# Sample attention in blocks of four heads, with page copies between the passes of the sums

## The reference, cut to what matters

```python
z = einsum('bqhd,bkhd->bhqk', q, k) * scale + bias
mask = key_pos[None, :] < qpos[:, None]
log_1mb = where(mask, log_sigmoid(-z), 0.0)
after = cumsum(log_1mb, axis=3, reverse=True) - log_1mb
w = where(mask, exp(log_sigmoid(z) + after), 0.0)
out = einsum('bhqk,bkhd->bqhd', w, v)
```

## Time and profile before

| what | value |
|---|---|
| median of 3 runs | 1071.79 us (1070.54 to 1072.94) |
| the profiled execution | 1072.91 us, its span 1071.2 us |
| PE busy over the span | 933.6 us (87%) |
| DVE, ACT busy | 635.5 us, 443.1 us |
| mean granted TensorE clock | 0.935 |

### The profile page before, as it was taken

One profiled execution on the slowest core, in us unless ns is written; L12 is line 12 of the kernel. 1 busy time (PEld: TensorE's weight loads), 2 busy tenths in 40 slices (PEclk: granted clock), 3 DMA queues, 4 the chain that ended last, 5 costly groups with the idle time before them and its releaser, 6 DMA issues.

```text
span 1071.2 us, 12096 instructions
## 1 busy us (share of the span) xinstructions
PE 933.6 (87%) x4149; PEld 674.0 (63%) x4149; DVE 635.5 (59%) x1206; ACT 443.1 (41%) x664; POOL 40.0 (4%) x75
## 2 busy tenths in 40 slices
PE   6799999999978687874769995999999999999695
PEld 3477676777745354442347684887887887787373
DVE  2319996011053753453354726888888888987774
ACT  0210112032223232332342222778778777777642
POOL 4000000300000000000000001000000000000300
PEclk9899999999966799997889997899999999999988
DMA  8042354424040386784602310899999999998601
GB/s 236 1 148 88 114 195 146 171 79 157 1 157 1 88 315 213 258 313 157 214 2 91 110 48 9 331 338 333 336 340 344 330 336 343 332 329 321 216 16 35
DMA packets 64211, 203.30 MB, mean 190 GB/s; under 512 B 8761, under 2 KB 9081, under 8 KB 60055
## 3 DMA queue, kind: packets, MB, share of 16 engines
q1 hardware_dynamic: 55424, 185.19, 48.3%
q10 hardware_dynamic: 6031, 9.19, 2.6%
q0 software_dynamic: 2704, 8.27, 2.5%
HBM read 188.96 MB, written 14.03 MB: 190 GB/s over the span
## 4 chain that ended last, share of the span: by engine, by line
PE 46%; DVE 12%; ACT 7%; issue 3%; DVEq 0%; ACTq 0%; POOL 0%
PE bank L1999 9%; PE bank L2001 8%; PE bank L2000 8%; PE bank L1990 5%; PE bank L2095 4%; PE bank L1921 3%; PE bank L1886 2%; PE bank L1895 2%; DVE last_piece L1494 2%; ACT pieces L627 1%; ACT att L627 1%; ACT last_piece L627 1%; DVE ring_lo L1469 1%; DVE scratch L1276 1%; PE bank L1839 1%
## 5 line engine op out<-in xcount | busy, mean ns | idle before, releaser
L1711 PE MATMUL bank<-scratch,ring 128*128 128x320 f32 x896 | 242.5, 433 | 0.0
L1711 PEld LDWEIGHTS bank<-scratch,ring 128*128 128x128 f32 x896 | 169.8, 190 | 70.6 <-issue 0.5
L1494 DVE TENSOR_TENSOR pieces<-ring,pieces 128x1024 fp32r<-128x1024 f32 x141 | 168.4, 1221 | 31.8 <-ACT pieces L627 29.7
L627 ACT ACTIVATE pieces<-ring 128x1024 fp32r<-128x1024 f32 x144 | 147.6, 1059 | 19.0 <-PE bank L2001 14.1
L627 ACT ACTIVATE proj<-bank 128x512 f32<-128x512 f32 (+4 forms) x73 | 36.3, 506 | 155.4 <-PE bank L1711 117.1
L1121 DVE SCALAR_TENSOR_TENSOR proj<-scratch,par_w,proj 128x256 f32<-128x256 f32 x240 | 73.7, 380 | 1.1
L1494 DVE TENSOR_TENSOR last_piece<-ring,last_piece 128x1024 fp32r<-128x1024 f32 x47 | 57.4, 1222 | 11.5 <-ACT last_piece L627 9.7
L627 ACT ACTIVATE last_piece<-ring 128x1024 fp32r<-128x1024 f32 x48 | 51.0, 1063 | 7.2 <-PE bank L2001 7.2
L627 ACT ACTIVATE scratch<-bank 128x512 f32<-128x512 f32 (+5 forms) x42 | 19.9, 520 | 73.2 <-PE bank L1921 35.5
L1886 PE MATMUL bank<-ident,ring 128*128 128x128 f32 x256 | 35.8, 302 | 13.9 <-ACT proj L627 6.2
L2095 PE MATMUL bank<-pick_t,h_tok 128*128 128x256 f32 x320 | 43.6, 295 | 3.1 <-DVE pick_t L1487 3.1
(11 more groups left out here) (386 smaller groups left out, 1660.2 us busy)
## 6 DMA issues: line engine op xcount, KB each, us to landing
ring<-in_w_expert_gate SPq DMA_DIRECT2D x16, 2048.0 KB, 7.7
ring<-in_w_expert_up SPq DMA_DIRECT2D x16, 2048.0 KB, 7.9
ring<-in_w_expert_down SPq DMA_DIRECT2D x16, 2048.0 KB, 7.9
ring<-in_w_in SPq DMA_DIRECT2D x14, 2048.0 KB, 7.9
ring<-in_cache_k SPq DMA_DIRECT2D x64, 256.0 KB, 5.1
ring<-in_cache_v SPq DMA_DIRECT2D x64, 256.0 KB, 5.5
moe_rows<-att ACTq DMA_DIRECT2D x16, 512.0 KB, 3.7
ring<-in_w_branch SPq DMA_DIRECT2D x3, 2048.0 KB, 9.2
```

Of the source, the lines that this page charges most:

```text
L627: return F(out, in_, ACT.Copy)
L1494: TT(piece_of[r % 4][:, 1, :], raw_piece(STEP + 3 * e, r), piece_of[r % 4][:, 0, :].bitcast(F32), ALU.subtract).then_inc(s("lo_ready"), 1)
L1711: m = MM(bank[t % 4][:, 0:T], slot(j, DC, GROUP)[:, k, (t % 4) * P:(t % 4 + 1) * P], h[:, k, :], start=k == 0, stop=k == DC - 1)
```

## The change

Three things are edited. First, the products of the sample attention are cut into blocks of four heads: request `u` and head group `g` have an output of 32 rows (`quarter(u, g)`), so the stationary tile has 32 columns and there are four such tiles side by side. A score block adds up only the two head pairs of its group; a value block has only the 256 value columns of its group. `o_rows` is 256 wide, and two transposes turn it instead of four. Second, VectorE's page copies 4 and 5 move into `later_sums`: copy 4 stands between the mask and the scan, copy 5 between the scan and the subtraction, and `mask_weight` moves behind copies 6 and 7. Third, ScalarE's `exp_weight` moves behind its page copies 4 and 5.

```diff
@@ ScalarE
                 k_copy(i, 2)
                 k_copy(i, 3)
-                exp_weight(i + (-1))
                 k_copy(i, 4)
                 k_copy(i, 5)
+                exp_weight(i + (-1))
                 biased(i, 0)
                 k_copy(i, 6)
                 k_copy(i, 7)
-                copy(o_rows, bank[7][:, :]).then_inc(s("turned_copied"), 1)
+                copy(o_rows, bank[7][:, 0:256]).then_inc(s("turned_copied"), 1)
@@ VectorE
-            def later_sums(i):
+            def later_sums(i, k_between=()):
...
                 ch(TT(probs[:, PAST:KEYS], probs[:, PAST:KEYS], mask_of(i), ALU.mult))
+                for k in k_between[0:1]:
+                    k_copy(i + 1, k)
                 ch(dve.tensor_tensor_scan(terms[:, KEYS - 1::-1], ones[:, 0:1].broadcast_to((P, KEYS)), probs[:, KEYS - 1::-1], 0.0, ALU.mult, ALU.add))
+                for k in k_between[1:2]:
+                    k_copy(i + 1, k)
                 TT(scores[:, 0:KEYS], scores[:, 0:KEYS], terms[:, 0:KEYS], ALU.subtract).then_inc(s("pw_arg"), 1)
...
-                later_sums(i + (-1))
-                k_copy(i, 4)
-                k_copy(i, 5)
-                mask_weight(i + (-1))
+                later_sums(i + (-1), (4, 5))
                 k_copy(i, 6)
                 k_copy(i, 7)
+                mask_weight(i + (-1))
                 outputs(i + (-1))
@@ TensorE
+            def quarter(u, g, at_=0):
+                return slice(at_ + u * DH + g * 32, at_ + u * DH + g * 32 + 32)
+
+            def own_queries(u, c):
+                return q_cur[:, u, c * 64 + c // 2 * 32:c * 64 + c // 2 * 32 + 32]
...
-                    for c in range(WC):
-                        for u in range(2):
-                            m = MM(bank[2 + hf][rows_of[u], :], q_cur[:, u, c * 64:(c + 1) * 64], k_feat[:, u, c, :],
-                                   start=c == 0, stop=c == WC - 1)
+                    for j in range(2):
+                        for g in range(2):
+                            for u in range(2):
+                                m = MM(bank[2 + hf][quarter(u, g), :], own_queries(u, 2 * g + j), k_feat[:, u, 2 * g + j, :],
+                                       start=j == 0, stop=j == 1)
...
-                    for u in range(2):
-                        m = MM(bank[7][u * DH:(u + 1) * DH, :], probs_t[:, p * P + u * DH:p * P + (u + 1) * DH],
-                               slot(first + u, NPAGE, W)[:, p, :] if p < NPAGE else v_tok[:, 2, :],
-                               start=p == 0, stop=p == NPAGE)
+                    for g in range(2):
+                        for u in range(2):
+                            v = slot(first + u, NPAGE, W)[:, p, :] if p < NPAGE else v_tok[:, 2, :]
+                            m = MM(bank[7][quarter(u, g), 0:256], probs_t[:, quarter(u, g, p * P)], v[:, 256 * g:256 * (g + 1)],
+                                   start=p == 0, stop=p == NPAGE)
...
-                for c in range(WC):
-                    m = TR(bank[1][:, c * P:(c + 1) * P], o_rows[:, c * P:(c + 1) * P], ident[:, :])
+                for j in range(2):
+                    m = TR(bank[1][:, j * P:(j + 1) * P], o_rows[:, j * P:(j + 1) * P], ident[:, :])
```

More of the change, by code:

```diff
@@ L201, in build @@
         probs_t = part(6016, KEYS + TS)
-        o_rows = part(7168, 512)
+        o_rows = part(7168, 256)
         k_feat = proj[:, TV:TX + WC + 1, :].rearrange("p c t -> p (c t)")[:, 0:4096].rearrange(
@@ L1294, in outputs @@
                         dve.tensor_copy(att[hf, c, bass.ds(i * (2 * NT) + SEQ, 2 * NT)].rearrange("p (u t) -> p u t", u=2),
-                                        bank[1][hf, c * P:(c + 1) * P].rearrange("p (u h t) -> p u h t", u=2, h=H)[:, :, 2 * c + e, :]
+                                        bank[1][hf, c % 2 * P:(c % 2 + 1) * P].rearrange(
+                                            "p (u g h t) -> p u g h t", u=2, g=2, h=4)[:, :, c // 2, 2 * (c % 2) + e, :]
                                         ).then_inc(s("o_copied"), 1)
@@ L1891, in score @@
                     pe.wait_ge(s("odd_copied"), i * 8 + (4 * hf + 6))
-                    rows_of = [slice(u * DH, (u + 1) * DH) for u in range(2)]
-                    for c in range(WC):
-                        for u in range(2):
-                            m = MM(bank[2 + hf][rows_of[u], :], q_cur[:, u, c * 64:(c + 1) * 64], k_feat[:, u, c, :],
-                                   start=c == 0, stop=c == WC - 1)
-                    if hf:
-                        for c in range(WC):
-                            for u in range(2):
-                                m = MM(bank[4][rows_of[u], 0:TS], q_cur[:, u, c * 64:(c + 1) * 64], proj[:, TK + c, SEQ:T],
-                                       start=c == 0, stop=c == WC - 1)
+                    for j in range(2):
[3 more added lines that the diff above has]
+                                       start=j == 0, stop=j == 1)
+                    if hf:
+                        for j in range(2):
+                            for g in range(2):
+                                for u in range(2):
+                                    m = MM(bank[4][quarter(u, g), 0:TS], own_queries(u, 2 * g + j), proj[:, TK + 2 * g + j, SEQ:T],
+                                           start=j == 0, stop=j == 1)
                     m.then_inc(s("z_done"), 1)
```

## The result

The changed kernel takes 1052.99 us, the median of 4 runs (1052.0 to 1054.26), beside 1071.35 us for the kernel before in the same series: a ratio of 0.983 [0.981, 0.985], 18.4 us faster. 1055 was forecast, with a range of 1047 to 1067. The profiled execution took 1054.26 us with a span of 1052.6; the kernel before took 1072.91 with 1071.2. The two spans differ by 18.6 us.

A forecast was written before the change was run, and what follows sets the result against it. No engine fills a loop turn; it hangs on VectorE and ScalarE, then on PE. Gains of 3.4 us ahead, three times 3.2 in the turns and 4.3 behind total 17.4: 1054.4, rounded up to 1055; range 1047 to 1067.

The forecast's parts named there:

- Products: Scores and value products: four tiles at a time double the rate, saving 1.71 us per score half and 3.84 for values.
- Rival B: Score and value products: four tiles share something and run at three quarters of the rate; 1064 us, chance 0.16.
- rival C: Score and value products: only two tiles run at a time, order's price stands alone; 11.7 us slower, 1083.5, chance 0.10.
- Loads: Weight loads of the value products: twice as many at 0.11 us, but hidden inside the products, so none counted.
- rival E: Weight loads: not hidden once there are four tiles; 27 us slower, 1099, chance 0.01.
- Small pieces: End of each pair: narrower `o_rows` copy saves 0.21 us, two fewer transposes 0.25, together 0.45 on the chain.
- The order: VectorE and ScalarE in a loop turn: VectorE waits at page copy 4, second scores start later, turn loses 1.07 us.
- The clock: PE behind the new gap before the second scores: granted clock falls to the low level, costing 1.70 us per turn.
- Rival A: PE behind the gap: clock stays high, three turns gain 1.7 us more; 1049 us, chance 0.12.
- The new keys: New-key products, 0.6 us: left as they are, being short and nearly all issue.
- Ahead of the loop and behind it: Two score halves ahead of the loop gain 3.4 us; last value products and small pieces behind it gain 4.3.
- Rival D: Stages behind the attention: gain given back because the granted clock falls there; within 0.2% of before, chance 0.03.

The follow-up runs named there:

- e7: Changed kernel with scores and values written as all of head group 0, then group 1, so stream neighbours use two tiles: 1064.45 us, ratio 0.993.
- e2: Kernel before with the new VectorE and ScalarE order alone, products still in blocks of eight heads: 1084.89 us, ratio 1.011.
- e3: Changed kernel with VectorE's old order; blocks of four heads and ScalarE's new order kept: 1038.9 us, ratio 0.969.
- e1: Changed kernel with the old order on both VectorE and ScalarE, leaving blocks of four heads alone: 1050.47 us, ratio 0.979.
- e5: Changed kernel with unread products filling TensorE's gap ahead of and behind page 7's turn in each loop turn: 1046.43 us, ratio 0.977.
- e6: e3 plus unread products: two at the end of each turn, 17 behind the loop ahead of the last weights' transposes: 1034.78 us, ratio 0.966.
- e4: Changed kernel with ScalarE's old order; blocks of four heads and VectorE's new order kept: 1062.8 us, ratio 0.990.

## Why the prediction was right, point by point

**Products.** Right. 16 records 1.92 us (1.7 and the ends, as foretold), values 4.14. Rival B, three quarters of the rate, would show 5.4 for the values, and rival C 8: both fall, and e7 shows what happens where the tiles don't run side by side.

**Loads.** The grouped lines give the loads of the value products:

```profile
L1935 PEld LDWEIGHTS bank<-ring,scratch x256: 106/110/178, 412.6 to 498.5; 128*32 128x32 f32 x128
```

64 of 0.11 us, 7.0 us together, lie inside 3.66 us of products, so rival E falls. By the rule of the Trainium skill that the prediction weighed ("TensorE: Matmul & The Clock Gate", section "Part 3: Packing small matmuls — row/col tiling"), that a load runs beside products in flight only where the row group differs, they would stand between the products. All tiles here use all 128 rows and the trace shows otherwise, so the measurement decides.

**Small pieces.** Right: the copy takes 0.38, and from it to the next turn it is 2.96 us against 3.39, 0.43 less (0.45 foretold).

**The order.** Right as a mechanism and in size. The wait at page copy 4 is 1.52 (1.4 foretold), the subtraction ends 433.56 - 425.27 = 8.29 behind the start of L1274 (8.3), ScalarE waits 4.18 (about 4), the second scores start 11.06 behind the first (11.2). The loss against before is 0.90 instead of 1.07. e2 confirms the price alone, e3 that VectorE's half of it is what costs.

**The clock.** Right as a mechanism, and the term of the sum that was mis-sized. From second scores to values the turn went from 6.22 to 6.99 us, where the sum had no change (1.71 less, 1.70 more). At full clock it is 4.25 (e1; 4.24 in e5), so the low clock costs 2.74 where the sum has 1.70, near the upper bound of 2.9: it covers the scores, the new keys and most of the weights' transposes, while the two rows that I took it from had a clock that was already between the levels. Rival A falls by the 0.50 in the stretches.

**The new keys.** At full clock the stretch is 1.97 shorter than before, where 1.71 was foretold for the scores alone. The prediction left the new keys as they are, "nearly all issue"; at full clock they fell from 0.66 us in the kernel before to 0.43 in e1.

**What the sum left out.** The turn's start. From the first transposes to the first scores it is 425.39 - 419.75 = 5.64 us against 6.83 in the earlier trace rows, 1.19 less, because the clock is high there now. I had carried the low start of the earlier trace rows over and put a second low stretch beside it; the second turn has one, and it has moved. So the 1.04 that the clock cost above its term was paid back by 1.19 here. With the pieces in order (turn's start, order, from second scores to values, values, small pieces): -1.19, +0.90, +0.77, -3.84, -0.43, together -3.79; foretold 0, +1.07, -0.01, -3.84, -0.45, together -3.2. Turn 1 shows the sum without this piece:

```profile
388.81 1.96 PE L1897 MATMUL bank<-ident,ring 128*128 128x128 f32 x16 [1.18 <-ACT scratch L766]
...
394.54 1.92 PE L1906 MATMUL bank<-proj,scratch 128*32 128x512 f32 x16 [0.88 <-DVE proj L1253]
```

It starts at full clock and takes 5.73 us to its scores, in the kernel before too (392.38 to 398.11), and it gained 2.5 where 3.2 was foretold. Turn 3 gained 0.5 more than turn 2 because in the kernel before its first half was the longest: 467.70 - 460.44 = 7.26 us to its scores, 0.43 more than in turn 2. In the changed kernel it takes 5.64 in both.

**Ahead of the loop and behind it.** 3.1 and 4.7 against 3.4 and 4.3, the sign of the second as argued: the saving falls on the part at full clock, and a little of the low part besides. **Rival D** falls: 18.4 of 18.6 us are kept.

The two largest errors of the sum cancelled by luck. From second scores to values the three turns take 7.04, 6.99 and 6.95 us, so over three turns the clock costs 3.1 us more than its term; the high clock at the start of turns 2 and 3, which the sum did not have, gives 2.8 back (1.19 and 7.26 - 5.64 = 1.62). Without the second the kernel would have taken some 1055.8 us, without the first some 1049.9. Both lie inside the range, so the range did not hang on the luck; but that the time came within 2 us says little about these two pieces. What stays open is why the same gap at a turn's end is followed by a high clock in the changed kernel (1.00 at 420) and by a low one in e3 and e5 (32 transposes 5.52 and 5.55 us): the runs show it, not its reason.

## What to carry to other kernels

Price the parts of a change apart, even where it comes as one: here the blocks gained some 22 us, and one of the two reorderings took 12 to 14 back and hid that the other is worth 10 to 12. An instruction that others wait for goes ahead of one that must itself wait on the same engine; that holds against the order of VectorE here and speaks for that of ScalarE. Where a short gap in a serial stage lowers the clock, count the products behind it at half speed, as scores, new keys and weights' transposes were here, look where the low stretch was before, and try unread products in the gap.

## What was not expected of the hardware

- Four tiles of 32 columns run at the full rate of one each with 0.11 us loads wholly hidden: 3.66 us for 64 value records, at full clock.
- TensorE takes a free tile's product ahead of waiting ones: 4 products away in e7's scores (1.94 us, four abreast), not 18 away in its values (7.18 us). How far it reaches between the two is open.
- Unread products pay for themselves: 6.6 us in e5. In e6 they take 4.4 us out of the sample attention; what of it reaches the end is less sure.
- The low stretches don't follow from one gap alone: in the second turn there is one in the kernels before and after, there are two in e1 and e4 and none in e6; the first turn of the kernel before has none.
